# Expert stage in units of 512 gate/up columns, with its pipeline running on across the expert boundary

## What is computed

```python
D_MODEL, N_EXPERTS, TOP_K, D_FF_EXPERT = 1024, 8, 2, 3584
logits = (t @ router).astype(jnp.float32)
top_v, top_i = lax.top_k(logits, TOP_K)
gates = jnp.sum(jax.nn.one_hot(top_i, N_EXPERTS) * softmax(top_v)[..., None], axis=-2)
for e in range(N_EXPERTS):
    g, u = jnp.split(t @ w_gu[e], 2, axis=-1)
    out = out + gates[:, e:e + 1] * ((jax.nn.silu(g) * u) @ w_down[e])
```

## Time and profile before

| | us |
|---|---|
| median of 3 runs | 1753.08 |
| lowest and highest | 1750.61, 1753.35 |
| span of the profiled execution | 1752.1 |
| of it: expert stage, from the first gate/up matmul | from 696.0 |
| PE, DVE, ACT busy in the span | 1564.9, 1231.9, 973.2 |

### The profile page before, as it was taken

One profiled execution on the slowest core, in us unless ns is written; L12 is line 12 of the kernel. 1 busy time (PEld: TensorE's weight loads), 2 busy tenths in 40 slices (PEclk: granted clock), 3 DMA queues, 4 the chain that ended last, 5 costly groups with the idle time before them and its releaser, 6 DMA issues.

```text
span 1752.1 us, 20909 instructions
## 1 busy us (share of the span) xinstructions
PE 1564.9 (89%) x7157; PEld 1235.7 (71%) x7157; DVE 1231.9 (70%) x1171; ACT 973.2 (56%) x978; POOL 18.6 (1%) x25
## 2 busy tenths in 40 slices
PE   3758878999598877999999999999999999999996
PEld 1536556888476555788788788788788788788784
DVE  1444555544558726788888888888888888888886
ACT  1232424443435533677677677676676776776673
POOL 0000000000000000000000000000000000000000
PEclk9778889999798977999999999999999999999998
DMA  7554685565344515899999999999999999999992
GB/s 273 184 189 173 221 277 175 190 192 192 120 145 144 199 41 192 284 362 334 315 366 335 316 366 336 318 366 333 318 366 336 308 366 334 324 366 318 327 364 100
DMA packets 340212, 471.62 MB, mean 269 GB/s; under 512 B 13023, under 2 KB 274861, under 8 KB 340158
## 3 DMA queue, kind: packets, MB, share of 16 engines
q1 hardware_dynamic: 336176, 464.43, 77.8%
q0 software_dynamic: 1216, 4.28, 0.7%
q10 hardware_dynamic: 2766, 2.22, 0.4%
HBM read 469.75 MB, written 1.13 MB: 269 GB/s over the span
## 4 chain that ended last, share of the span: by engine, by line
PE 82%; DVE 10%; ACT 4%; DMA 2%; issue 1%; ACTq 0%; POOL 0%; DVEq 0%; POOLq 0%
PE bank L1395 23%; PE bank L1397 23%; PE bank L1396 23%; DVE low L1307 2%; PE bank L1407 2%; PE bank L1770 2%; ACT high L741 2%; PE bank L1884 2%; PE bank L1912 1%; DVE low L814 1%; DVE hid L1159 1%; PE bank L1424 1%; DMA x<-x_sample 1%; PE bank L1443 1%; ACT high L468 1%
## 5 line engine op out<-in xcount | busy, mean ns | idle before, releaser
L1307 DVE TENSOR_TENSOR low<-raw,high 128x2048 fp32r<-128x2048 f32 x333 | 760.6, 2292 | 150.5 <-ACT high L741 137.6
L741 ACT ACTIVATE high<-raw 128x2048 fp32r<-128x2048 f32 x333 | 634.6, 1915 | 111.9 <-PE bank L1397 111.3
L1395 PE MATMUL bank<-high,slotH 128*128 128x512 f32 x896 | 359.1, 401 | 26.2 <-DVE low L1307 25.4
L1397 PE MATMUL bank<-high,slotL 128*128 128x512 f32 x896 | 356.9, 398 | 0.0
L1396 PE MATMUL bank<-low,slotH 128*128 128x512 f32 x896 | 356.0, 397 | 0.0
L1395 PE MATMUL bank<-high,upH 128*128 128x512 f32 (+1 forms) x550 | 227.6, 414 | 4.4 <-DVE upL L944 2.8
L1395 PEld LDWEIGHTS bank<-high,slotH 128*128 128x128 f32 x896 | 169.1, 189 | 73.7 <-DVE low L1307 33.8
L1397 PE MATMUL bank<-high,upL 128*128 128x512 f32 (+1 forms) x550 | 217.3, 395 | 0.0
L1396 PE MATMUL bank<-low,upH 128*128 128x512 f32 (+1 forms) x550 | 215.3, 391 | 0.0
L814 DVE TENSOR_TENSOR low<-raw,high 128x2048 fp32r<-128x2048 f32 (+3 forms) x59 | 132.3, 2250 | 106.8 <-ACT high L468 106.6
L1397 PEld LDWEIGHTS bank<-high,slotL 128*128 128x128 f32 x896 | 169.3, 189 | 40.8
(11 more groups left out here) (228 smaller groups left out, 1221.2 us busy)
## 6 DMA issues: line engine op xcount, KB each, us to landing
raw<-moe_gu SPq DMA_DIRECT2D x448, 512.0 KB, 5.4
raw<-moe_down SPq DMA_DIRECT2D x112, 1024.0 KB, 6.6
raw<-ada_w SPq DMA_DIRECT2D x48, 1024.0 KB, 7.0
raw<-ffn_gu SPq DMA_DIRECT2D x44, 512.0 KB, 4.9
raw<-ffn_down SPq DMA_DIRECT2D x11, 1024.0 KB, 4.9
raw<-conv_pw SPq DMA_DIRECT2D x16, 512.0 KB, 4.4
raw<-w_in SPq DMA_DIRECT2D x6, 1024.0 KB, 8.0
raw<-w_o SPq DMA_DIRECT2D x4, 1024.0 KB, 6.8
```

The costliest lines, as they stand in the source:

```text
L741: a.activation(high[:, m % SPLITS, :], raw[:, n % RAWS, :], ACT.Copy).then_inc(S("high_ready"), 1)
L1307: v.tensor_tensor(low[:, m % SPLITS, :], raw[:, n % RAWS, :], high[:, m % SPLITS, :].bitcast(F32), ALU.subtract).then_inc(S("low_ready"), 1)
L1395: pe.matmul(out, xh, wh, start=start, stop=False)
L1397: return pe.matmul(out, xl, wh, start=False, stop=stop)
```

## The change

- Units have 512 hidden columns: seven an expert. A gate/up unit has four pieces (`"g", u, q`: two blocks of rows, 512 gate and 512 up columns, rows of 2 KB in memory), the down weights of a unit two (`"d", u, w`). It is 42 pieces of 1 MB as before, two loads for a g piece and one for a d piece.
- Gate and up have a bank each (0 and 1, or 2 and 3), the transposes bank 4, the down product banks 5 and 6, the transposed `pickR` bank 7. The silu, `up`, `act_high` and `act_low` work on 128 x 512 in one instruction; `eact`, `e_upH` and `e_upL` have one buffer.
- The stream of pieces runs across experts: each loop round of expert e has the last two down units of expert e - 1 (`"p"`), split around its first gate/up unit. Expert 0 is written out ahead of the loop (`head`), the last down units behind it (`tail`).
- The silu of unit u - 1 follows the first piece of unit u on ACT. The scatter of expert e - 1 stands in unit 1 of expert e, its gated adds in two pairs in that unit.
- `pick_of` writes `pickR` itself and ACT's copy of it goes. ACT's copy to `backR` is a function `back`, which stands in unit 3 behind its fourth gate/up piece, as the transposes do on PE.

The core of the diff: the stream, then the loads, then ACT, DVE and PE.

```diff
+UE = 512
+UCE = UE // P
+UNITS_E = D_FFE // UE
+LAST_E = UNITS_E - 1
+SCATTER = (5, 6, 7, 0)
+QE = KT // 2
...
+    def unit(u):
+        return [("g", u, q) for q in range(QE)]
+    def down(kind, u):
+        return [(kind, u, 0), (kind, u, 1)]
+    middle = []
+    for u in range(1, LAST_E):
+        middle += unit(u) + down("d", u - 1)
+    head = unit(0) + middle + unit(LAST_E)
+    loop = down("p", LAST_E - 1) + unit(0) + down("p", LAST_E) + middle + unit(LAST_E)
+    return head, loop, down("p", LAST_E - 1) + down("p", LAST_E)
...
+                if kind == "g":
+                    v = t["moe_gu"][0].rearrange("e (q k p) n -> e q p k n", p=P, k=2)[bass.ds(e, 1), w]
+                    dst = w_slot(raw, slot, (2, 2, UE))
+                    c0 = u * UE
+                    sp.dma_start(dst[:, :, 0, :], v[:, :, :, c0:c0 + UE]).then_inc(arrived, 16)
+                    sp.dma_start(dst[:, :, 1, :], v[:, :, :, D_FFE + c0:D_FFE + c0 + UE]).then_inc(arrived, 16)
...
+                    src = t["moe_down"][0].rearrange("e (u w c p) n -> e u w p c n", p=P, c=2, w=2)
+                    of = e if kind == "d" else e - 1
+                    sp.dma_start(w_slot(raw, slot, (2, D)), src[bass.ds(of, 1), u, w]).then_inc(arrived, 16)
...
-                def picked(e):
-                    a.wait_ge(S("pick_ready"), e + (ge + 1))
-                    a.activation(pickR[:, :, :], pick[:, :, :], ACT.Copy).then_inc(S("pickR_ready"), 1)
...
+                def silu(e, where, u):
+                    a.wait_ge(S("piece_used"), e * PER_E + (split + NUM_E[where][("g", u, QE - 1)] + 1))
+                    a.activation(eact[:, :], bank[:, 2 * (u % 2), :], ACT.Silu).then_inc(S("e_silu"), 1)
...
+                def back(e):
+                    a.wait_ge(S("back_T"), e + (ge + 1))
+                    a.activation(cat(backR[:, :, :]), bank[:, 7, 0:TILES * P], ACT.Copy).then_inc(
+                        S("back_ready"), 1)
+                def units(e, where):
                     for u in range(1, UNITS_E):
-                        if u + 1 < UNITS_E:
-                            part(e, "a", u + 1)
-                        silu(e, u)
+                        part(e, where, "g", u, 0)
+                        silu(e, where, u - 1)
+                        part(e, where, "g", u, 1)
+                        if u == 1 and where == "loop":
+                            out_high(e - 1, "loop")
+                        part(e, where, "g", u, 2)
+                        part(e, where, "g", u, 3)
                         if u == 3:
-                            a.wait_ge(S("back_T"), e + (ge + 1))
-                            a.activation(cat(backR[:, :, :]), bank[:, 6, 0:TILES * P], ACT.Copy).then_inc(
-                                S("back_ready"), 1)
...
+                            back(e)
+                        if u < LAST_E:
+                            part(e, where, "d", u - 1, 0)
+                            act_high(e, u - 1)
+                            part(e, where, "d", u - 1, 1)
...
+                part(0, "head", "g", 0, 3)
+                units(0, "head")
+                with a.Fori(1, EXPERTS) as e:
+                    part(e, "loop", "p", LAST_E - 1, 0)
+                    act_high(e - 1, LAST_E - 1)
+                    part(e, "loop", "p", LAST_E - 1, 1)
+                    part(e, "loop", "g", 0, 0)
+                    silu(e - 1, "loop", LAST_E)
+                    gather_out(e)
+                    for q in range(1, QE):
+                        part(e, "loop", "g", 0, q)
+                    part(e, "loop", "p", LAST_E, 0)
+                    act_high(e - 1, LAST_E)
+                    part(e, "loop", "p", LAST_E, 1)
+                    units(e, "loop")
...
+                def act_low(e, u):
+                    v.wait_ge(S("e_high"), e * UNITS_E + (ge * UNITS_E + u + 1))
+                    v.tensor_tensor(e_upL, bank[:, 4, :], e_upH.bitcast(F32), ALU.subtract).then_inc(S("e_low"), 1)
...
+                def units(e, where):
+                    for u in range(1, UNITS_E):
+                        part(e, where, "g", u, 0)
+                        up(e, u - 1)
+                        part(e, where, "g", u, 1)
+                        if u == 1 and where == "loop":
+                            out_low(e - 1)
+                        part(e, where, "g", u, 2)
+                        part(e, where, "g", u, 3)
+                        if u == 1 and where == "loop":
+                            gated(e - 1, 0)
+                        if u < LAST_E:
+                            part(e, where, "d", u - 1, 0)
+                            act_low(e, u - 1)
+                            part(e, where, "d", u - 1, 1)
+                        if u == 1 and where == "loop":
+                            gated(e - 1, 1)
...
+                with v.Fori(1, EXPERTS) as e:
+                    v.wait_ge(S("back_T"), e + ge)
+                    pick_of(e)
+                    part(e, "loop", "p", LAST_E - 1, 0)
+                    act_low(e - 1, LAST_E - 1)
+                    part(e, "loop", "p", LAST_E - 1, 1)
+                    part(e, "loop", "g", 0, 0)
+                    up(e - 1, LAST_E)
+                    for q in range(1, QE):
+                        part(e, "loop", "g", 0, q)
+                    part(e, "loop", "p", LAST_E, 0)
+                    act_low(e - 1, LAST_E)
+                    part(e, "loop", "p", LAST_E, 1)
+                    units(e, "loop")
...
+                def e_down(e, where, kind, u):
+                    for w in range(2):
+                        n = ready(e, where, (kind, u, w))
+                        wh, wl = w_slot(high, n, (2, D)), w_slot(low, n, (2, D))
+                        of = e - 1 if kind == "p" else e
+                        if w == 0:
+                            pe.wait_ge(S("e_low"), of * UNITS_E + (ge * UNITS_E + u + 1))
...
+                def units(e, where):
+                    for u in range(1, UNITS_E):
+                        if u == 2:
+                            pe.wait_ge(S("y_part"), e * 4 + (4 * ge + 1))
+                        gate_up(e, where, u, 0)
+                        gate_up(e, where, u, 1)
+                        e_T(e, u - 1)
+                        if u == 1 and where == "loop":
+                            scatter(e - 1)
+                        gate_up(e, where, u, 2)
+                        gate_up(e, where, u, 3)
+                        if u == 3:
+                            for tt in range(TILES):
+                                last = pe.transpose(bank[:, 7, tt * P:(tt + 1) * P], pickR[:, tt, :].bitcast(F32),
+                                                    ident)
+                            last.then_inc(S("back_T"), 1)
+                        if u == 1 and where == "loop":
+                            pe.wait_ge(S("y_part"), e * 4 + (4 * ge - 1))
+                        if u < LAST_E:
+                            e_down(e, where, "d", u - 1)
...
+                with pe.Fori(1, EXPERTS) as e:
+                    pe.wait_ge(S("back_ready"), e + ge)
+                    pe.wait_ge(S("e_low"), e * UNITS_E + (ge * UNITS_E - 1))
+                    gather(e)
+                    e_down(e, "loop", "p", LAST_E - 1)
+                    pe.wait_ge(S("e_act"), e * UNITS_E + ge * UNITS_E)
+                    pe.wait_ge(S("slot_ready"), e * 4 + (4 * ge + 4))
+                    gate_up(e, "loop", 0, 0)
+                    gate_up(e, "loop", 0, 1)
+                    e_T(e - 1, LAST_E)
+                    gate_up(e, "loop", 0, 2)
+                    gate_up(e, "loop", 0, 3)
+                    e_down(e, "loop", "p", LAST_E)
+                    units(e, "loop")
+                e_down(EXPERTS, "tail", "p", LAST_E - 1)
+                e_T(EXPERTS - 1, LAST_E)
+                e_down(EXPERTS, "tail", "p", LAST_E)
+                scatter(EXPERTS - 1)
```

More of the change, by code:

```diff
@@ L356, in experts, with free @@
[L356 to L361, removed]
+                def free(e, part, piece):
+                    sp.wait_ge(S("low_ready"), e * PER_E + (split + NUM_E[part][piece] - RAWS + 1))
@@ new lines, in experts @@
+                for i, piece in enumerate(HEAD_E):
+                    if passes == 0 and i < RAWS:
+                        last = ORDER[first + i - RAWS]
+                        if last in DNUM:
+                            sp.wait_ge(S("direct_used"), DNUM[last] + 1)
+                        else:
+                            sp.wait_ge(S("low_ready"), NUM[last] + 1)
+                    else:
+                        free(0, "head", piece)
+                    expert_load(0, first, "head", piece)
@@ L363, in _ @@
+                with sp.Fori(1, EXPERTS) as e:
+                    for piece in LOOP_E:
+                        free(e, "loop", piece)
+                        expert_load(e, first, "loop", piece)
+                for piece in TAIL_E:
+                    free(EXPERTS, "tail", piece)
```

(20 more changed lines are left out.)

326 lines of the change are left out of this document (125 added, 201 removed).

## The result

The changed kernel takes 1782.76 us (median of 4 runs, 1781.13 to 1783.54) against 1751.84 us for the kernel before in the same comparison (1744.18 to 1753.35): a ratio of 1.0194, 95% interval 1.0169 to 1.0218. It is 31 us slower; 1779.2 was forecast, in a range of 1764 to 1791, as 26.1 more than before. The profiled execution has a span of 1780.3 us and took 1782.11.

What follows compares the result with a forecast made beforehand. The prediction took PE work plus 17 holes as the bound, not transfers. Unit 3 +27.8, boundary -12.3, clock +10.2 and head +0.4 gave +26.1 on a span of 1752.1, so 1779.2 us, range 1764 to 1791.

Steps and rivals of the forecast that it cites:

- The deciding term: Unit 3: `back` waits ahead of d2.0's high part, so PE loses 5.45 us instead of 1.97; +27.8 us over 8 experts.
- The boundary: Between experts: silu follows the next unit's first piece, so the boundary hole and the small ones go; -12.3 us.
- the cover of 1.1 us: Ring of pieces: a 4.49 us chain against 5.62 us of PE work hides the wider ACT and DVE steps; cost 0.
- Rival D: Wider silu/act steps on DVE outgrow the cover, 0.3 us in each of 56 units, +17: 1796 us; chance 0.08.
- The clock: After each unit-3 idle: PE at half clock for 3.4 us, 1.7 us lost an expert; +10.2 us net, bounds included.
- The sum: Whole kernel: 27.8 - 12.3 + 10.2 + 0.4 = +26.1 us on the span; an expert takes 133.4 us.
- The head's hole: First expert: silu of unit 0 holds up g1.1, 2.2 us lost against 1.6 + 0.17 before; +0.4 us.
- 2 KB rows: Weight loads: wider packets move more per share, but nobody waits for them; 0 us.
- The bound of 14 us: PE's matmul speed: wider packets could give back 1.5% of 943 us, or lose as much; taken as 0.
- Rival B: Unit 3: the stall comes but the clock stays up, +12.5 us: 1765.6 us; chance 0.11.
- C: Boundary gain comes and unit 3 costs no more than now, if `back` didn't hold the ring: 1741.2 us; chance 0.05.

Runs made afterwards that it cites:

- first experiment: The changed kernel with ACT's `back` moved from unit 3 to unit 4, behind the silu of unit 3: 1717.59 us, ratio 0.983 to the kernel before.
- second experiment: The changed kernel with `back` one step later on ACT, behind the high part of d2.0: 1739.81 us, ratio 0.9937 to the kernel before.
- filled run: The changed kernel with 21 extra PE matmuls, results never read, in the hole of unit 3: 1761.39 us, ratio 1.0081 to the kernel before.
- fourth experiment: The changed kernel with `back` in unit 4 and gate/up weights loaded in rows of 1 KB again: 1719.85 us, ratio 0.9825 to the kernel before.

## Why the prediction was right

- **The deciding term.** 5.45 us lost at unit 3 was forecast, 5.53 measured (1021.56 to 1027.09); `back` waited 7.16 us where I said near 6.8, the idle is 5.29 where I said 5.2, ended by act_low as said. Moving `back` alone (first experiment) and by one step (second) shows it as cause, not only as neighbour.
- **The boundary.** Both boundary losses went, as laid out; no new hole appeared, so the cover of 1.1 us held under the wider steps. Rival D is out.
- **The clock.** I took 1.7 us an expert with bounds of 0 and 2.0; it is 1.95. The term was right in kind and too small: I priced 3.4 us of half clock, while each stretch of it lasted 6.8 us, of which 4.1 fell on work. The Trainium skill ("TensorE: Matmul & The Clock Gate", Terms) prices a throttled stretch at half its time; for the 4.1 us in which PE had work that is an estimate of 2.05, and the trace agrees (1.95 by the filled run). Taken for the whole 6.8 us it would be 3.4, which the run doesn't bear out.
- **The sum.** 133.4 us an expert forecast, 133.1 measured. Two misses cancel there: the clock and the hole were 0.3 more, and PE's own work 0.6 less, which I had at zero (part of it is explained at the end). Outside the experts I missed more. The head's hole was 2.0 us idle as said, but I had not priced that the clock falls behind it (1.7 us). It falls behind the idle ahead of the end too (another 1.7), and that idle is 1.94 us where 1.67 was:

```profile
1754.16 0.47 PE L1461 MATMUL bank<-high,upH 128*128 128x512 f32 x1 [1.94 <-DVE upL L1366]
...
1754.90:1758.20 3.30, 3.30 (x9) 2.56 (x8) 0.00 (x0) 0.00 (x0) 0.00 (x0) 0.50 0.00 0
```

- **A term that I didn't have.** Behind the last gated add DVE idles longer ahead of its four closing steps, before and after:

```profile
DVE hid L1381 <- issue: 1.5, 1, 1.5
```

```profile
DVE hid L1447 <- issue: 3.8, 1, 3.8
```

That is 2.3 us; all six kernels with the new loop have 3.8 to 4.1 there, and the three with the old one 1.5. The profile shows nothing that DVE waits for, so the cause stays open. With these the stage should have grown by 26.1 + 0.6 + 2.0 + 1.7 + 1.7 + 0.3 + 2.3 - 4.7 = 30.0 us (hole and clock of eight experts, head, tail twice, DVE, PE's work); it grew by 30.1. The span grew by 28.2, since the stage began 1.9 us earlier in this profile. The path through unit 3 was foreseen; that the total came within 4 us of the forecast is in part luck, terms missed on both sides.
- **2 KB rows.** Zero, as taken. The bound of 14 us either way was too wide and wrongly founded: the 452 and 267 records that it compares hold 20 and 14 matmuls of 128 columns, so they aren't step rates. Nor is the step the same in all pieces, as the end of this document shows. The fourth experiment closes the term.
- **Rival B** (the clock stays up) is what the filled run makes: 131.2 us an expert. C, the faster side, would have needed `back` off the path, and the first experiment is that kernel: 1717.6. My price for C, 1741, assumed that the hole of unit 3 stays as it was; I didn't see that the same wait cost 1.97 us an expert needlessly already.

## What to carry to other kernels

Where several engines hand pieces through a short ring, every step that stands in an engine's program ahead of a ring piece and waits for a consumer further on puts that wait into the ring. Look for an engine's longest wait on a side product (here a 128 x 256 copy, 0.4 us of work) and ask which piece stands behind it; moving it behind a piece that waits for the same thing anyway cost nothing here. Do that before building wider units or longer pipelines: two moved steps gave the old kernel 32 us, and all of the new structure another 3 to 4.

## What the runs showed of the hardware

A long idle costs twice: after each of the eight idles of 5.29 us TensorE ran at half clock for 4.1 us of work, 1.95 us lost. Of shorter ones the length alone doesn't decide: none of the eight idles of 1.78 us (second experiment) was followed by a fall, two of the eight of 1.80 in the kernel before were; the start's idle of 2.0 us was in each of the five kernels that had it; the idle of 1.93 or 1.94 ahead of the end was in one of six, the changed kernel.

Down pieces that follow another down piece ran a little faster, which I can't explain. In the changed kernel, starts of the first down piece, the second, and the next gate/up piece:

```profile
1046.24 0.40 PE L1461 MATMUL bank<-high,upH 128*128 128x512 f32 x1
...
1049.00 0.39 PE L1461 MATMUL bank<-high,upH 128*128 128x512 f32 x1
...
1051.72 0.39 PE L1461 MATMUL bank<-high,slotH 128*128 128x512 f32 x1
```

2.76 us, then 2.72, while two gate/up pieces took 5.62 in the earlier trace rows. The kernel before has it too, in its only pair of down pieces an expert, 2.82 and 2.73:

```profile
820.21 0.44 PE L1395 MATMUL bank<-high,upH 128*128 128x512 f32 x1
...
823.03 0.39 PE L1395 MATMUL bank<-high,upH 128*128 128x512 f32 x1
...
825.76 0.39 PE L1395 MATMUL bank<-high,slotH 128*128 128x512 f32 x1
```

The fourth experiment has the same 125.6 us with gate/up packets half as long, so it isn't their size. Seven pairs an expert instead of one, at some 0.05 us for each second piece, account for about 0.3 of the 0.7 us an expert that the wide units bring; the rest, and what makes a step 0.227 or 0.234 us, stays open.
